# Two PSUM banks of a chunk filled side by side, and the squares for the head norms split into two fp32r parts

## What is computed

```
h = rmsnorm(x, g_pre);  u = h @ w_in            # 2048 -> 16,192 columns
qn = rmsnorm(qa[.., :128]) ...                  # branch A: low rank, norms over heads
bq = rope(rmsnorm(b_q.reshape(.., 8, 2, 64)))   # branch B: norm over 64 features, also for keys
cq = rmsnorm(c_q.reshape(.., 8, 128))           # branch C: norm over 128 features, also for keys
o  = softmax(mask(q k^T)) v                     # per branch and head
y  = sum_n sigmoid(gate_n) * ((o_n * silu(z_n)) @ w_branch[n]);   x = x + y @ w_out
```

## Time and profile before

| | us |
|---|---|
| median of 3 runs | 3213.33 |
| the profiled execution's own time | 3216.58 |
| its span, first to last instruction | 3214.6 |
| TensorE busy with matmuls | 3183.0 (99%) |
| VectorE busy | 2096.1 (65%) |
| ScalarE busy | 1721.8 (54%) |
| mean busy share of the 16 DMA engines | 57.5% |

### The profile page before, as it was taken

How to read it: one execution, slowest core, us unless ns; L and a number is a source line. 1 busy time by engine, 2 the same in 40 slices (tenths; PEclk the granted TensorE clock), 3 DMA queues, 4 the chain that set the end, 5 groups by cost and what they waited for, 6 DMA issues and landing times.

```text
span 3214.6 us, 52057 instructions
## 1 busy us (share of the span) xinstructions
PE 3183.0 (99%) x18246; PEld 2759.5 (86%) x18246; DVE 2096.1 (65%) x2694; ACT 1721.8 (54%) x2264; POOL 0.2 (0%) x4
## 2 busy tenths in 40 slices
PE   8999999999999899999999999999999999999999
PEld 7888888888888788888888888888888888888888
DVE  7677565666657776666666555776766666655574
ACT  5685434444445556655555555544664555555553
POOL 0000000000000000000000000000000000000000
PEclk9999999999999999999999999999999999999999
DMA  7656555555556555565556555565556555665555
GB/s 224 189 167 196 194 184 171 186 165 180 182 160 211 169 169 156 158 190 176 158 181 186 169 183 175 179 200 173 151 155 198 163 175 161 188 188 176 173 183 170
DMA packets 569759, 571.64 MB, mean 178 GB/s; under 512 B 26304, under 2 KB 565440, under 8 KB 569664
## 3 DMA queue, kind: packets, MB, share of 16 engines
q1 hardware_dynamic: 569664, 570.42, 57.5%
HBM read 568.25 MB, written 2.10 MB: 177 GB/s over the span
## 4 chain that ended last, share of the span: by engine, by line
PE 95%; DVE 2%; ACT 1%; DMA 1%; issue 1%; SPq 0%; DVEq 0%; ACTq 0%
PE pg L480 89%; PE pa L616 1%; PE pa L649 1%; PE pa L666 1%; DVE hl L1114 1%; PE pa L656 1%; PE pa L667 0%; PE pa L587 0%; ACT hl L809 0%; PE pa L625 0%; ACT corr L817 0%; DMA xres<-x 0%; PE pa L755 0%; DMA raw<-w_o 0%; DVE uT L1187 0%
## 5 line engine op out<-in xcount | busy, mean ns | idle before, releaser
L480 PE MATMUL pg<-hT,hl 128*128 128x512 f32 x11456 | 2055.7, 340 | 0.8 <-DVE hl L1114 0.8
L480 PEld LDWEIGHTS pg<-hT,hl 128*128 128x128 f32 x11456 | 1752.7, 188 | 265.4 <-issue 9.2
L1114 DVE TENSOR_TENSOR hl<-raw,hl 128x1024 fp32r<-128x1024 f32 x1072 | 1259.3, 1209 | 376.5 <-ACT hl L809 371.0
L809 ACT ACTIVATE hl<-raw 128x1024 fp32r<-128x1024 f32 x1072 | 1085.1, 1043 | 343.1 <-PE pg L480 330.7
L480 PE MATMUL pg<-uT,hl 128*128 128x256 f32 (+1 forms) x3712 | 642.0, 334 | 23.0 <-DVE hl L1114 14.5
L480 PEld LDWEIGHTS pg<-uT,hl 128*128 128x128 f32 x3712 | 558.7, 189 | 101.8 <-DVE hl L1114 15.7
L817 ACT ACTIVATE corr<-pg 128x512 f32<-128x512 f32 (+1 forms) x288 | 171.4, 595 | 875.6 <-PE pg L480 875.6
L480 PE MATMUL pg<-hl,hT 128*128 128x512 f32 (+1 forms) x1792 | 327.1, 341 | 0.0
L480 PEld LDWEIGHTS pg<-hl,hT 128*128 128x128 f32 x1792 | 274.8, 188 | 47.0 <-issue 7.7
L1121 DVE TENSOR_TENSOR work<-pg,corr 128x512 f32<-128x512 f32 (+1 forms) x154 | 105.8, 687 | 319.1 <-ACT corr L817 318.7
L1121 DVE TENSOR_TENSOR gat<-pg,corr 128x512 f32 (+1 forms) x72 | 49.6, 689 | 154.2 <-ACT corr L817 154.2
(11 more groups left out here) (164 smaller groups left out, 1326.5 us busy)
## 6 DMA issues: line engine op xcount, KB each, us to landing
raw<-w_in SPq DMA_DIRECT2D x792, 512.0 KB, 4.6
raw<-w_br SPq DMA_DIRECT2D x96, 512.0 KB, 4.3
raw<-w_out SPq DMA_DIRECT2D x64, 512.0 KB, 4.8
raw<-w_rnn SPq DMA_DIRECT2D x32, 512.0 KB, 4.7
raw<-w_o SPq DMA_DIRECT2D x32, 512.0 KB, 5.4
raw<-w_att SPq DMA_DIRECT2D x16, 512.0 KB, 4.1
raw<-w_uq SPq DMA_DIRECT2D x16, 384.0 KB, 3.5
tab<-tabs SPq DMA_DIRECT2D x5, 896.0 KB, 7.6
```

The lines of the kernel that those rows point to most:

```text
L480: return nc.tensor.matmul(out, lhsT, rhs, start=start, stop=stop, skip_group_check=True)
L809: nc.scalar.activation(hl4[:, j % 2, 0, a:a + n], raw[:, bass.ds(j % 2 * UC + a, n)], ACT.Copy)\
L1114: tt(hl4[:, j % 2, 1, a:a + n], raw[:, bass.ds(j % 2 * UC + a, n)], hl4[:, j % 2, 0, a:a + n].bitcast(F32), ALU.subtract).then_inc(lo_done, 1)
```

## The change

The two banks of a chunk are filled side by side. For each tile k the two 512-column matmuls go first, one into each bank, then the two 256-column matmuls: 512, 512, 256, 256. This holds for all forms with two banks; the narrow chunk of branch A's rotary key has one bank (`subs` is 1) and keeps its order. The operands, the number of matmuls and of weight loads, and the semaphores around a half stay as they were.

```diff
-            def feature_major(bank, wh, wl, op, ks, start, stop, base=0):
+            def feature_major(b, subs, wh, wl, op, ks, start, stop, base):
                 for n, k in enumerate(ks):
-                    mm(pg3[:, bank, :], wh[:, k - base], op[:, k, :], start and n == 0, False)
-                    ins = mm(pg3[:, bank, S:], wl[:, k - base], op[:, k, 0:S], False, stop and n == len(ks) - 1)
+                    for s in range(subs):
+                        mm(pg3[:, b + s, :], wh[:, k - base, s * P:s * P + P], op[:, k, :], start and n == 0, False)
+                    for s in range(subs):
+                        ins = mm(pg3[:, b + s, S:], wl[:, k - base, s * P:s * P + P], op[:, k, 0:S], False,
+                                 stop and n == len(ks) - 1)
                 return ins
-            def token_major(bank, tok, hiw, low, both, op, ks, start, stop, base):
+            def token_major(b, hiw, both, op, ks, start, stop, base):
                 for n, k in enumerate(ks):
-                    mm(pg3[:, bank, :], op[:, k, tok * P:tok * P + P], both[:, k - base], start and n == 0, False)
-                    ins = mm(pg3[:, bank, S:], op[:, k, S + tok * P:S + tok * P + P], hiw[:, k - base], False,
-                             stop and n == len(ks) - 1)
+                    for s in range(2):
+                        mm(pg3[:, b + s, :], op[:, k, s * P:s * P + P], both[:, k - base], start and n == 0, False)
+                    for s in range(2):
+                        ins = mm(pg3[:, b + s, S:], op[:, k, S + s * P:S + s * P + P], hiw[:, k - base], False,
+                                 stop and n == len(ks) - 1)
                 return ins
```

```diff
+        sums_of_r = {"B": u3[:, 15, P:2 * P], "C": u3[:, 15, 0:P]}
+        sq_parts = [u3[:, 8 + 2 * h:10 + 2 * h, :].rearrange("p a (b n) -> p (a b) n", b=2) for h in range(2)]
...
-            def squares_sum(kind):
-                red = blk if kind == "B" else ones
+            def squares_sum(kind, l):
+                if kind in "BC":
+                    pe.wait_ge(ones_ready, l + 1)
+                    for b in range(2):
+                        for h in range(2):
+                            ins = mm(pa3[:, b, :], sums_of_r[kind], u3[:, 8 + 2 * h + b, :], h == 0, h == 1)
+                    ins.then_inc(norm_done, 1)
+                    return
...
                         if kind in "BC" and j == 3 and what == "u":     # ScalarE
+                            hi(u, 5, (0,))
                             act.wait_ge(evac_done, c + 2 + 2)
                             act.wait_ge(u_ready, 2 * pi)
-                            nc.scalar.activation(nt3[:, 0:4, :], qk_l[:, 0:4, :], ACT.Square).then_inc(sq_ready, 1)
+                            steps.done(nc.scalar.activation(nt3[:, 0:4, :], qk_l[:, 0:4, :], ACT.Square))
+                            nc.scalar.activation(sq_parts[0], nt3[:, 0:4, :], ACT.Copy).then_inc(sq_hi, 1)
+                            halves = (1,)
+                        hi(u, n + 2, halves)
...
+                        nc.scalar.activation(u3[:, 15, 0:S], cst[:, P:3 * P], ACT.Copy).then_inc(ones_ready, 1)
...
+                        if kind in "BC" and j == 3 and what == "u":     # VectorE
+                            lo(u, 5, (0,))
+                            dve.wait_ge(sq_hi, pi - 4 * l - 8 + 1)
+                            tt(sq_parts[1], nt3[:, 0:4, :], sq_parts[0].bitcast(F32), ALU.subtract).then_inc(sq_ready, 1)
+                            halves = (1,)
                         lo(u, n + 2, halves)
```

More of the change, by code:

```diff
@@ L246, in build @@
         g_sig = sem("g_sig")
-        z_sig, sq_ready, norm_done, r_ready, normed, rot_done, qk_ready = (
-            sem(n) for n in ("z_sig", "sq_ready", "norm_done", "r_ready", "normed", "rot_done", "qk_ready"))
+        z_sig, sq_hi, sq_ready, ones_ready, norm_done, r_ready, normed, rot_done, qk_ready = (
+            sem(n) for n in ("z_sig", "sq_hi", "sq_ready", "ones_ready", "norm_done", "r_ready", "normed", "rot_done", "qk_ready"))
         scores_done, max_ready, exp_done, probs_ready, tr_done, pt_ready, pv_done = (
@@ L529, in unit @@
                             ready(ks)
[L530 to L538, removed]
+                        b, begin, end = 2 * (cj % 2), start and n == 0, stop and n == len(parts) - 1
+                        if form == "r":
+                            ins = feature_major(b, subs, wh[:, h], wl[:, h], op, ks, begin, end, base + 4 * h)
+                        elif form == "t":
+                            ins = token_major(b, wh, both_view(j, CH), op, ks, begin, end, base)
+                        else:
+                            ins = feature_major(b, subs, wh, wl, op, ks, begin, end, base)
                     ins.then_inc(half_done, 1)
@@ L609, in rotate @@
                     .then_inc(rot_done, 1)
-            def squares_sum(kind):
-                red = blk if kind == "B" else ones
-                if kind == "A":
-                    nc.tensor.matmul(pa3[:, 2, 0:S], blk, nt3[:, 4, :], start=True, stop=True)
+            def squares_sum(kind, l):
[6 more added lines that the diff above has]
+                    return
+                nc.tensor.matmul(pa3[:, 2, 0:S], blk, nt3[:, 4, :], start=True, stop=True)
                 for b in range(2):
-                    ins = nc.tensor.matmul(pa3[:, b, :], red, nt3[:, 2 * b:2 * b + 2, :].rearrange("p t n -> p (t n)"),
+                    ins = nc.tensor.matmul(pa3[:, b, :], ones, nt3[:, 2 * b:2 * b + 2, :].rearrange("p t n -> p (t n)"),
                                            start=True, stop=True)
@@ L731, in pair @@
                         pe.wait_ge(sq_ready, pi - 4 + 1)
-                        squares_sum(kind)
+                        squares_sum(kind, l)
                     elif what == "rot":
@@ L995, in pair @@
                                 copy_corr(u + n, c + cc, cc)
-                        hi(u, n + 2, halves)
                         if kind in "BC" and j == 3 and what == "u":
+                            hi(u, 5, (0,))
                             act.wait_ge(evac_done, c + 2 + 2)
                             act.wait_ge(u_ready, 2 * pi)
-                            nc.scalar.activation(nt3[:, 0:4, :], qk_l[:, 0:4, :], ACT.Square).then_inc(sq_ready, 1)
+                            steps.done(nc.scalar.activation(nt3[:, 0:4, :], qk_l[:, 0:4, :], ACT.Square))
+                            nc.scalar.activation(sq_parts[0], nt3[:, 0:4, :], ACT.Copy).then_inc(sq_hi, 1)
+                            halves = (1,)
+                        hi(u, n + 2, halves)
                         if kind in "BC" and j == 7 and what == "u":
@@ L1598, in _ @@
                     tt(sq_new[:, 0, :], sq_sum[:, 0, :], sq_sum[:, 1, :], ALU.add).then_inc(n_sum, 1)
-ACT_PAIR_STEPS = {"A": 2, "B": 3, "C": 1}
+ACT_PAIR_STEPS = {"A": 2, "B": 4, "C": 2}
 def tables():
```

## The result

The changed kernel takes 3186.10 us (median of 4 runs, 3185.69 to 3186.26) against 3213.95 us before (4 runs, 3212.29 to 3215.07) on the same chip: ratio 0.9914, 95% interval 0.9896 to 0.9931. That is 27.9 us or 0.9% faster, about twice the 12.8 us that were forecast. The time lies inside the stated range (3165 to 3223), the sign was right, the size was not.

A forecast was written before the change was run, and what follows sets the result against it. The prediction took the kernel to be bound by TensorE's matmul count times their distance. From the profiled 3216.6 us, -12.8 (sums of squares) + 0 (order) gave 3203.8, or 3200.5 us for the median; range 3165 to 3223 us.

The forecast's parts named there:

- What bounds the kernel: Whole kernel: time is the number of matmuls times their distance on TensorE, 8288 pairs at 0.3503 us.
- the prediction's own sign: Projections: the prediction is wrong if the pair's distance moves by more than 0.001 us on the mean.
- The sums of squares: 16 norms of B and C: 1.72 us of fp32 matmuls become 0.90 to 0.93 us of fp32r, saving 12.8 us.
- the replay: One norm followed through ScalarE and VectorE: the added subtraction ends 0.4 to 0.5 us before TensorE asks for it.
- Rival three: Norms of B and C: TensorE waits for the split squares, 8 to 16 us come back, about 3212 us; chance 0.12.
- The side-by-side order: All projections: reordering two banks' matmuls changes only neighbours; taken as zero, bounds -41 to +22 us.
- the two rhythms: Projection stretches before: a 512- and 256-column pair takes 0.3454 us (cheap) or 0.3529 us (dear) at full clock.
- One: Projections: the cheap rhythm takes over, -41 us, about 3160 us, half of it 3180; chance 0.22 in full or part.
- Two: All projections: the dear rhythm takes over, +22 - 13 = +9 us, 3222 us; chance 0.16.
- Four: Projections: the clock swings, a tenth of the pairs at half clock, +290 us, 3490 us; chance 0.02.
- the rule cited for it: Trainium skill on PSUM depth-cycling: changing bank at every matmul could make TensorE's clock swing between both levels.
- Five: Long matmuls come down to the fp32 sum's pass rate, 0.215 us: -230 us, 2970 us; chance 0.03.

The follow-up runs named there:

- one_bank: Changed kernel, but banks filled one after the other, with 512, 512, 256, 256 made of two tiles k of one bank: 3185.56 us, ratio to before 0.9913.
- alt_banks: Changed kernel, but per tile k 512 and 256 into the first bank, then 512 and 256 into the second: 3201.41 us, ratio to before 0.9960.
- runs8: Changed kernel, but all eight 512-column matmuls of a half unit, then all eight of 256: 3192.01 us, ratio to before 0.9933.
- order_only: Kernel before with only the new side-by-side order, squares still summed in fp32: 3199.42 us, ratio to before 0.9955.
- shifted: Changed kernel, but bank by bank, in the order 512, 256, 256, 512 over each two tiles k: 3185.66 us, ratio to before 0.9906.
- runs4: Changed kernel, but four 512-column matmuls (two tiles k, both banks), then four of 256: 3201.37 us, ratio to before 0.9965.
- odd_rounds: Changed kernel, but only the first and third tile of each half unit as 512, 512, 256, 256, the others alternating: 3208.73 us, ratio to before 0.9984.
- one_round: Changed kernel, but only the first tile k of each half unit as 512, 512, 256, 256, the other three alternating: 3196.17 us, ratio to before 0.9942.
- all_short: Changed kernel, but every 512-column projection matmul made as two of 256, each with its own weight load: 3289.34 us, ratio to before 1.0236.
- norm_only: Changed kernel with the matmul order of before, keeping only the split squares: 3202.56 us, ratio to before 0.9966.

## Why the prediction was wrong, point by point

**What bounds the kernel** was right, and so was the sentence that a thousandth of a microsecond a pair is 8.3 us. By the prediction's own sign it failed: the pair went from 0.3503 to 0.3474 us, and it had called itself wrong from 0.001 us on.

**The sums of squares** were right in each term: 1.72 us removed, 0.92 added (0.90 to 0.93 forecast), 12.8 us in the profile, 11.4 us by runs (7.7 to 14.1 by interval). No wait arose, and the spare 0.43 us was what the replay gave. Rival three can be dropped.

**The side-by-side order** is the step that failed: the term was put at zero, and it is 14.5 us by runs (19.7 us in the profiled executions). It was a term with bounds from -41 to +22 us, and I took zero because "all neighbours that are in the trace cost the same". They don't, as the two rhythms themselves showed. In the runs the changed order takes 2.787 us a half unit everywhere, where the old one takes 2.773 or 2.827 us, 2.806 in the mean. The forecast had its sign from the norms alone; to the order's share it gave none. The reasoning on the banks (eight into one bank and then eight into the other cost nothing) was right, and one_bank and alt_banks prove it; but the same was concluded for the neighbours by length, from one row of short ones (0.120 us) and the fp32 sum. A price for each kind of neighbour doesn't exist: one and the same step from a long to a long matmul takes 0.232 or 0.233 us here and 0.227 within the runs of runs8, and no count of changes gives the order of the table. What decides is the whole sequence of lengths. "The distance isn't fixed by the instructions alone, but by how the stream falls into step after a stall" was right for the old order and became untrue with the new one: in the four profiled executions with LL SS (order_only, changed, one_bank, shifted) nearly every half unit without a stall took 2.787 us.

**Rivals.** One came about in part: the two rhythms gave way to a third, single one, 0.014 us a half unit above the cheap one and 0.04 below the dear one. I had priced this half-way case at 3180 us, beside a forecast of 3200.5. Its stated reason, that the step between unequal lengths is halved, isn't the reason: runs4 and runs8 halve it further and are slower. Two (the dear rhythm takes over) didn't happen here, but nearly did to a close neighbour: odd_rounds falls into a step of 2.813 us nearly everywhere and takes up half of what the norms save. Three didn't happen: TensorE has no wait for L1444. Four: the granted clock was 1.00 in all stretches shown, with a change of bank at every matmul, also in alt_banks at every second; the rule cited for it met nothing here. Five fell: 0.226 us is the least lasting distance of 512-column fp32r matmuls in any order tried, above the 0.215 us taken for an fp32 pass.

**Could the size have been foreseen?** The trace of before gave the fixed part (0.120 us for 256 columns) and both rhythms. It didn't give what a new sequence would do, and seven more sequences of lengths later there is no rule for it. Zero stood for the mean of the old order's two rhythms; no row spoke for the new sequence.

**Open.** What makes the losses multiples of 0.0067 us; why LL SS holds its step behind any stall and L S doesn't. That the sequence of lengths makes the difference is shown; how the engine comes to its step isn't. No order tried stays at 2.773 us; the 14 us between 2.773 and 2.787 weren't won. No run beats the changed kernel; one_bank and shifted are within 0.6 us of it.

## What to carry to other kernels

When matmuls of two lengths make up a stream that fills TensorE, their sequence is a parameter worth some tenths of a per cent, and it can't be argued out: try the few sequences, and look at counts in equal windows of the trace and at the spread of repeated runs: 15 runs spread over 12 us before, 12 runs of three kernels with the new sequence over 1.5 us. Where two lengths turn up in a histogram, look whether they take turns before calling them two states (one_round did). Split a change that does two things (banks and lengths here) before crediting the one it is named for. A sum over many tokens that is done in plain fp32 can go to two fp32r parts if the splitting engines have a slot, and that gain can be worked out from the rows of one instance (here 12.8 us by replay, 11.4 us by runs, interval 7.7 to 14.1).

## What the runs showed of the hardware

- fp32r matmuls, each with its weight load, at full granted clock: 0.1067 + 0.0133 us for 256 columns (all_short) and 0.2133 + 0.0133 us for 512 (runs8) in runs of one length. Plain fp32 records, with a weight load each, have 0.43 us for 512 columns and 0.109 us for 128 (L666 of the changed kernel). If a record is two passes, its columns at 2.4 GHz take 0.427 and 0.107 us, and only 0.002 to 0.003 us is over. As such a record with its weight load goes by in 0.109 us, less than the 0.120 of the short fp32r matmul, the fixed part is not the weight load as such. The Trainium skill ("TensorE: Matmul & The Clock Gate", section "Back-to-back issue gap") has 2.5 ns over the columns, for a matmul in isolation; the fp32 rows agree with the figure, the fp32r ones don't.
- At a granted clock of 0.50 the same fp32r matmuls of before stand 0.427 and 0.213 us apart (1103 to 1105.5 us), which is 512 and 256 columns at 1.2 GHz with nothing over. So in these few matmuls the fixed part of 0.013 us isn't there.
- The same matmuls, alternating 512 and 256 columns, run in either of two rhythms, 2% apart (348 matmuls in 60 us in before, 341 in norm_only, 1020 to 1080 us), at the same clock and a DMA share of 0.58 in both. The choice is kept through hundreds of matmuls: it changes 3 times in before where one half unit follows another directly, and else where other matmuls or a stall lie between.
- The bank that a matmul writes into, the one before it or another, made no difference in three pairs of kernels (norm_only and alt_banks, changed and one_bank, runs4 and one_bank8: 1.2, 0.5 and 0.8 us apart).
